# Second mixer: score groups issued between the two halves of a state drive, on other rows of the array

## Chip, core and metric

One core of a Trainium2 chip runs the whole program. The metric is the device time of one execution in microseconds, lower is better. TensorE (PE) does the matrix products, VectorE (DVE), ScalarE (ACT) and GpSimd (POOL) the element work, and SyncE (SP) issues the loads of the weights.

## What is computed

Two transformer layers with 256 tokens and width 1024 (`first_block`), then a third layer (`second_block`), all in float32. The change is in the mixer of the third layer, which has three branches over one input `h`:

```python
qa, ka, va, u, qm, km, vm, gates = split_in(h @ w_in[l])
oa = swa_attention(qa, ka, va, sinks[l], slopes_swa)       # 8 heads of 64, 2 key heads
ys = s5_ssm(u, ...)                                        # 32 groups x 64 complex states
om = moba_attention(qm, km, vm, slopes_moba)               # 8 heads of 64, 2 key heads
mixed = g[0] * (oa @ w_o_swa) + g[1] * (glu(gelu(ys)) @ w_o_ssm) + g[2] * (om @ w_o_moba)
```

In the state branch each group drives 64 complex states from 16 inputs. Two groups fill 128 partitions of states, so the 32 groups make 16 blocks. A block's drive is a product over 32 rows (two groups of 16 inputs), once for the real and once for the imaginary part. A scan over the 256 tokens follows, and a product over 128 rows that projects the states back.

## The kernel before

**Weights.** Every weight is loaded as `raw`, rounded by ACT to `whi` (L1029), and the rest is formed by DVE as `wlo` (L1563). PE then runs three products for each (L432, L433, L434). A piece is 1024 columns of one weight; DVE and ACT prepare a piece two ahead of PE (`AHEAD`), in three buffers.

**The strips of the second mixer.** `MIXED` lists 40 pieces, s = 0 to 39: the keys, the queries, six gate matrices of four pieces each (`gate2` is s = 28 to 31, `gate3` s = 32 to 35) and the first output projection. Tables say at which s something else is done beside the piece, and PE, ACT, DVE and POOL each walk through s in order:

- `SCORED_AT`: an attention item, that is 4 heads of 128 x 128 scores or 2 heads of 128 x 256, in one PSUM bank (`score`, L553). Items 0 to 5 are of `sA`, 6 to 11 of `mA`. The heads of an item are all even or all odd, so that its products all read rows 0 to 63, or all rows 64 to 127. DVE adds the bias and takes the maximum (L1731 on), ACT takes exponentials (L1109), PE transposes them one strip later (`prob_turn`, L538), ACT copies them (L1122), and PE multiplies by the values three strips after the scores (`weigh`, L566).
- `DRIVEN_AT`: a block of the state (`drive`, L939), two products of 32 rows x 256 columns in one bank. Block jj of four reads rows 32 jj to 32 jj + 31. DVE multiplies by phases (`turn_back`, L2356 and L2357), POOL adds (L2576 and L2577), DVE scans and multiplies at the next strip (`turn_forth`), POOL adds again, and PE projects four strips after the drive (`project`, L951).
- `ZIN_AT`: at s = 30 ACT takes the gelu of the first three quarters of the state branch's output (L1476, L1479).

Scores stand at odd s (7 to 29) and drives at even s (2 to 32). A turning bank of three (b3 to b5) takes scores, drives and transposes in turn; the strips use b0 to b2, two at a time, so that the second bank of a new strip group is the first bank of the one before: ACT must have emptied it (L1440 for a gate) before PE's fourth product of the new group.

The phases are built once, early in the program, by POOL (`phase_table`, L2509 and on): four blocks at a time, in DRAM until they are needed.

A float32 product like L553 or L939 is two instructions on PE in the trace (one for each half of the numbers), and the trace names the shape of the array that it uses: `64*128` is 64 rows by 128 columns.

The first mixer has a place where 64-row products on the two halves of the array follow each other: its differential scores (`diff_score`, L724), first the two or four products on rows 0 to 63, then those on rows 64 to 127. After the first of these groups comes a transpose of an 8-row tile on rows 0 to 7 (L749), array shape 32 x 128.

Of the kernel before, what the change touches and what calls it, by code (L numbers as in the profile page):

```python
# [13 lines left out]
P = 128  # L14
# [301 lines left out]

STRIP_END = {name: s + 1 for s, (name, n) in enumerate(MIXED)}

SCORED_AT = {7 + 2 * i: i for i in range(12)}
DRIVEN_AT = {2 + 2 * k: k for k in range(16)}  # L320
SWA_OUT, MOBA_OUT = 22, 34

ZIN_AT = {30: (0, 1, 2), 37: (3,)}
LAM_INIT = 0.8 - 0.6 * math.exp(-0.3 * 0)
# [75 lines left out]
def pe_program(K, G, A):  # L400

    S, T = K.S, K.nc.tensor
    pe = Engine(T)
    ident, banks = K.ident, K.banks
    free = [()] * 8
# [136 lines left out]
    def probs_ready(name, i):  # L542
        pe.wait_ge(*S.copied_a.at(("p", name, i)))

    def score(a, i, ready):
        t, heads = ITEMS[i]
        nk = P * (t + 1)
        b = turn_bank()
        K.place["s", a.name, i] = b
        for event in ready:  # L550
            pe.wait_ge(*event)
        for k, h in enumerate(heads):
            ins = T.matmul(banks[b][:, k * nk:(k + 1) * nk], a.queries(h, t), a.keys(h, nk), start=True, stop=True)  # L553
        ins.then_inc(*S.scored.done((a.name, i)))
        free[b] = (S.biased.at((a.name, i)),)
# [317 lines left out]
    def second():  # L873
        pairs[0], pair_n[0] = ((1, 2), (0, 1), (2, 0)), 1
        gemm("su", S.copied_d.at(("su", 0)), S.copied_d.at(("su", 1)), None, {0: lambda: norm_turns("s", "f3", True, (2, 3))})
        b = turn_bank()
        K.place["spread"] = b
        for t in range(2):
            pe.wait_ge(*S.rstd.at(("s", t)))
            ins = T.matmul(banks[b][:, P * t:P * t + P], K.stat(("y", "s"), 2)[:, t:t + 1].to_broadcast([P, P]), ident,  # L880
                           start=True, stop=True)
        ins.then_inc(*S.turned.done("spread"))
        free[b] = (S.copied_a.at("spread"),)

        def keys_piece(name, n):

            if n == 0:
                K.place[name] = next_pair()
            pair = K.place[name]
            hi, lo, j = piece("w_in_2", 0, 4 * n, 4, [({"ka": 512, "km": 1792}[name], 256)])  # L890
            K.at[name, n] = j
            for kk in range(4):
                kt = 4 * n + kk
                open_bank(pair[0])
                ins = products(banks[pair[0]][:, 0:256], (hi[:, kk, 0:P], lo[:, kk, 0:P]), wide(K.hT)(kt), kt == 0, kt == 7)
                if kt == 7:
                    ins.then_inc(*S.dense.done((name, 0)))
            for kk in range(4):
                kt = 4 * n + kk
                open_bank(pair[1])  # L900
                for t in range(2):
                    ins = products(banks[pair[1]][:, P * t:P * t + P], both(K.hT)(kt, t), (hi[:, kk, P:256], lo[:, kk, P:256]),
                                   kt == 0 and t == 0, kt == 7, True)
            ins.then_inc(*S.dense.done(("w", j), *([(name, 1)] if n else [])))
            if n:
                free[pair[0]], free[pair[1]] = (S.copied_d.at((name, 0)),), (S.copied_a.at((name, 1)),)

        def mixed_piece(name, n):
            if name in ("ka", "km"):
                keys_piece(name, n)  # L910
                return
            gemm_piece(G[name], n)
            if n == G[name].n - 1:
                for t in range(2):
                    free[K.place[name][t]] = ((S.gate.at((int(name[4]), t)) if name[:4] == "gate" else
                                               S.gated.at((0, int(name[3]), t)) if name[:3] == "swa" else S.copied_a.at((name, t))),)

        def ready(i):
            q, k = ("sqm", "km") if i >= 6 else ("sqa", "ka")
            return list(copied(q)) + [S.copied_d.at((k, 0)), S.keys[k].at(0)], [S.copied_a.at((k, 1))]  # L920

        def outputs_turn(J):
            b = turn_bank()
            K.place["out", J] = b
            pe.wait_ge(*S.cl.at(0))
            for ri in range(2):
                ins = T.transpose(banks[b][:, P * ri:P * ri + P], K.CL[ri][:, J, :], ident)
            ins.then_inc(*S.turned.done(("out", J)))
            free[b] = (S.proj.at(J),)

        def drive(k):
            J, jj = divmod(k, 4)
            b = turn_bank()
            K.place["drive", k] = b
            for t in range(2):
                pe.wait_ge(*S.copied_d.at(("su", t)))
            pe.wait_ge(*S.bt.at(1))
            for ri in range(2):
                ins = T.matmul(banks[b][:, 256 * ri:256 * ri + 256], K.BT[32 * jj:32 * jj + 32, ri, J, :],  # L939
                               K.uT[32 * jj:32 * jj + 32, J, :], start=True, stop=True)  # L940
            ins.then_inc(*S.driven.done(k))
            free[b] = (S.back.at(k),)

        def project(k):
            J, jj = divmod(k, 4)
            if jj == 0:
                open_bank(6)
            pe.wait_ge(*S.proj.at(J))
            pe.wait_ge(*S.turned_forth.at(k))
            for ri in range(2):  # L950
                ins = T.matmul(banks[6][:, 0:256], K.CR[:, J % 2, ri, P * jj:P * jj + P], K.state[k % 3][:, ri, :],  # L951
                               start=(jj == 0 and ri == 0), stop=(jj == 3 and ri == 1))
            ins.then_inc(*S.projected.done(k))
            if jj == 3:
                free[6] = (S.scan.at(("z", J)),)
                if J + 2 < 4:
                    outputs_turn(J + 2)
        for s, (name, n) in enumerate(MIXED):
            if s in SCORED_AT:
                i = SCORED_AT[s]  # L960
                score(A["mA" if i >= 6 else "sA"], i % 6, ready(i)[0])
            if s in DRIVEN_AT:
                drive(DRIVEN_AT[s])
            mixed_piece(name, n)
            if s == 1:
                outputs_turn(0)
                outputs_turn(1)
            if s - 4 in DRIVEN_AT:
                project(DRIVEN_AT[s - 4])
            if s - 3 in SCORED_AT:  # L970
                i = SCORED_AT[s - 3]
                weigh(A["mA" if i >= 6 else "sA"], i % 6, ready(i)[1])
            if s - 1 in SCORED_AT:
                i = SCORED_AT[s - 1]
                prob_turn("mA" if i >= 6 else "sA", i % 6, 4)
            if s in (SWA_OUT, SWA_OUT + 1):
                out_turn("sA", 0, K.O, lambda t, g: S.weighed.at(("sA", t)), (s - SWA_OUT,))
            if s in (MOBA_OUT, MOBA_OUT + 1):
                out_turn("mA", 0, K.O, lambda t, g: S.weighed.at(("mA", t)), (s - MOBA_OUT,))

        def gated(branch):
            return [[S.gated.at((branch, c, t)) for t in range(2)] for c in range(2)]
        pairs[0] = ((2, 0), (1, 3))
        gemm("glu1", S.silu.at(("glu", 0)), S.silu.at(("glu", 1)))
        gemm("glu0", S.product.at(("glu", 0)), S.product.at(("glu", 1)))
        gemm("moba0", *gated(2)[0])
        gemm("ssm0", *gated(1)[0])

        def out_of(c, g):
            out_turn(f"s{c}", 512 * c, K.M, lambda t, g: S.gated.at((1, c, t, g)), (g,))  # L990
        gemm("moba1", *gated(2)[1], None, {1: lambda: out_of(0, 0)})
        gemm("ssm1", *gated(1)[1], None, {0: lambda: out_of(0, 1)})
        project_x("s", "so", "f4", (0, 1, 2, 3), {1: lambda: out_of(1, 0), 2: lambda: out_of(1, 1)})
# [555 lines left out]
def dve_program(K, G, A):  # L1549
# [298 lines left out]
    SM = K.SM  # L1848
# [441 lines left out]
    def second():  # L2290
# [67 lines left out]

        def turn_forth(k):
            X, T = K.state[k % 3], K.spin[k % 2]  # L2360
            mg = SM[:, 1, k:k + 1].to_broadcast([P, 256])
            dve.wait_ge(*S.turned_back.at(k))
            if k:
                dve.wait_ge(*S.forth.at(k - 1))
            for a in range(2):
                V.tensor_tensor_scan(K.G[:, a, :], mg, X[:, a, :], 0.0, ALU.mult, ALU.add).then_inc(*S.dve_own.done())
            before()
            c, s = phases(k)
            V.tensor_tensor(T[:, 0], K.G, c, ALU.mult).then_inc(*S.dve_own.done())
            V.tensor_tensor(T[:, 1], K.G, s, ALU.mult).then_inc(*S.forth.done(k))  # L2370
# [102 lines left out]
def pool_program(K, G, A):  # L2473
# [28 lines left out]
    def phase_table(J):  # L2502
# [3 lines left out]
        if J >= 2:  # L2506
            pool.wait_ge(*S.spilled[J - 2].at(0))
        for ri in range(2):
            E.tensor_copy(tab[:, ri, :, 0:1], K.SM[:, 2 + ri, 4 * J:4 * J + 4].unsqueeze(2)).then_inc(*S.pool_own.done())  # L2509
        n = 1  # L2510
        while n < 256:
            c, s = tab[:, 0, :, 0:n], tab[:, 1, :, 0:n]
# [196 lines left out]
```

## Time and profile before

| | |
|---|---|
| median of 3 runs | 1677.44 us (1676.97 to 1677.71) |
| the profiled execution, its own time | 1676.27 us |
| its span in the trace | 1674.8 us |
| PE busy, share of the span | 99% |
| DVE, ACT, POOL | 66%, 52%, 14% |
| granted TensorE clock | 0.997 |
| second mixer in the trace | about 1250 to 1440 us |

A busy PE here means that some product was in the pipeline. Products overlap in the trace, since each stays in the pipeline after the next has begun; so the cost of one is read from the distance between the starts of two, not from its length.

### The profile page before, as it was taken

To read this page: it belongs to the slowest core of one execution; us is meant where nothing else is said; L and a number is where in the kernel's file an instruction comes from. 1 tells how busy PE (TensorE), PEld (TensorE's weight loads), DVE (VectorE), ACT (ScalarE), POOL (GpSimd) and SP (SyncE) were. 2 spreads that over 40 slices of the span, in tenths; PEclk is the share of its full clock that TensorE was granted. 3 is DMA by queue.
4 is the path that set the end of the run, shared out by engine and by line. 5 is a ranking of instruction groups with operands and counts; after the bars stand their busy time and mean duration, and the time that the engine had idled before them with its cause. 6 is when DMAs were issued, how large, how long until landed. Compare 5 with 4: busy or idle time off the path is not lost.

```text
span 1674.8 us, 21348 instructions
## 1 busy us (share of the span) xinstructions
PE 1652.0 (99%) x8136; PEld 1376.2 (82%) x8136; DVE 1102.3 (66%) x1744; ACT 864.4 (52%) x1323; POOL 236.4 (14%) x343
## 2 busy tenths in 40 slices
PE   7999999999999999999999999999999999999997
PEld 6888887788888888888889888888898778888886
DVE  5766788767656556555776685655568887775555
ACT  5555457665555445444544555544444446454444
POOL 2499701000000000000000000000044343100000
PEclk9999999999999999999999999999999999999999
DMA  8666755444455565655654453555574434555552
GB/s 250 203 214 202 228 158 186 144 140 138 146 195 179 187 187 177 189 188 189 201 163 141 162 162 123 183 187 189 188 237 141 134 120 136 187 191 189 189 180 97
DMA packets 185248, 293.05 MB, mean 175 GB/s; under 512 B 13527, under 2 KB 106234, under 8 KB 184250
## 3 DMA queue, kind: packets, MB, share of 16 engines
q1 hardware_dynamic: 180288, 274.81, 51.2%
q0 software_dynamic: 4368, 16.29, 3.1%
q8 instruction: 64, 1.05, 0.2%
q10 hardware_dynamic: 490, 0.59, 0.1%
q14 instruction: 38, 0.31, 0.1%
HBM read 286.12 MB, written 5.25 MB: 174 GB/s over the span
## 4 chain that ended last, share of the span: by engine, by line
PE 93%; DVE 4%; ACT 2%; issue 1%; ACTq 0%; DVEq 0%
PE b L432 28%; PE b L434 27%; PE b L433 27%; PE b L590 2%; PE b L553 1%; DVE wlo L1563 1%; PE b L566 1%; PE b L496 1%; PE b L939 1%; PE b L800 1%; PE b L951 1%; PE b L816 1%; PE b L538 1%; PE b L512 1%; ACT whi L1029 1%
## 5 line engine op out<-in xcount | busy, mean ns | idle before, releaser
L1563 DVE TENSOR_TENSOR wlo<-raw,whi 128x1024 fp32r<-128x1024 f32 (+1 forms) x523 | 653.3, 1252 | 465.3 <-ACT whi L1029 464.6
L1029 ACT ACTIVATE whi<-raw 128x1024 fp32r<-128x1024 f32 (+1 forms) x523 | 550.1, 1053 | 578.8 <-PE b L434 576.2
L432 PE MATMUL b<-whi,hT 128*128 128x512 f32 (+1 forms) x1184 | 468.9, 396 | 1.9 <-DVE wlo L1563 1.9
L434 PE MATMUL b<-whi,hT 128*128 128x512 f32 (+1 forms) x1184 | 459.0, 388 | 0.0
L433 PE MATMUL b<-wlo,hT 128*128 128x512 f32 (+1 forms) x1184 | 458.1, 387 | 0.0
L432 PEld LDWEIGHTS b<-whi,hT 128*128 128x128 f32 x1184 | 222.8, 188 | 53.1 <-issue 7.1
L432 PE MATMUL b<-whi,oT 128*128 128x512 f32 x672 | 264.8, 394 | 0.0
L434 PE MATMUL b<-whi,oT 128*128 128x512 f32 x672 | 261.9, 390 | 0.0
L433 PE MATMUL b<-wlo,oT 128*128 128x512 f32 x672 | 261.5, 389 | 0.0
L434 PEld LDWEIGHTS b<-whi,hT 128*128 128x128 f32 x1184 | 222.7, 188 | 46.7
L433 PEld LDWEIGHTS b<-wlo,hT 128*128 128x128 f32 x1184 | 223.1, 188 | 42.2 <-issue 0.5
L434 PEld LDWEIGHTS b<-whi,oT 128*128 128x128 f32 x672 | 126.1, 188 | 26.6
L433 PEld LDWEIGHTS b<-wlo,oT 128*128 128x128 f32 x672 | 126.3, 188 | 25.5
L432 PEld LDWEIGHTS b<-whi,oT 128*128 128x128 f32 x672 | 126.2, 188 | 25.4
L1109 ACT ACTIVATE R<-R,st 128x256 f32<-128x256 f32 (+1 forms) x96 | 43.5, 455 | 69.7 <-DVE st L1736 30.4
L2601 POOL DMA_DIRECT2D biasB<-in_rel x1 | 0.9, 917 | 494.9 <-PE b L590 494.9
L1156 ACT ACTIVATE biasA<-b,st 128x256 f32<-128x256 f32 x88 | 41.1, 475 | 44.1 <-PE b L434 42.8
L432 PE MATMUL b<-hT,whi 128*128 128x256 f32 (+1 forms) x216 | 62.8, 291 | 0.0
L433 PE MATMUL b<-hT,whi 128*128 128x256 f32 (+1 forms) x216 | 61.0, 282 | 0.0
L434 PE MATMUL b<-hT,wlo 128*128 128x256 f32 (+1 forms) x216 | 61.0, 282 | 0.0
L1644 DVE TENSOR_TENSOR oT<-b,oT 128x512 fp32r<-128x512 f32 x80 | 53.5, 683 | 9.4 <-ACT oT L1131 5.0
L2553 POOL DMA_DIRECT2D biasA<-in_alibi x1 | 0.5, 540 | 407.2 <-DVE biasB L1811 407.2
(315 smaller groups left out, 1782.2 us busy)
## 6 DMA issues: line engine op xcount, KB each, us to landing
raw<-in_ffn_w_in SPq DMA_DIRECT2D x350, 256.0 KB, 3.0
raw<-in_ffn_w_out SPq DMA_DIRECT2D x88, 512.0 KB, 3.3
raw<-in_w_ff SPq DMA_DIRECT2D x64, 512.0 KB, 3.3
raw<-in_w_in SPq DMA_DIRECT2D x40, 512.0 KB, 3.6
raw<-in_x_w_kv SPq DMA_DIRECT2D x32, 512.0 KB, 3.5
raw<-in_even_w_in SPq DMA_DIRECT2D x24, 512.0 KB, 4.1
raw<-in_odd_w_in SPq DMA_DIRECT2D x24, 512.0 KB, 3.8
raw<-in_x_w_q SPq DMA_DIRECT2D x16, 512.0 KB, 3.9
```

Source lines behind the costliest of these rows:

```text
L432: T.matmul(out, ah, bh, start=start, stop=False, skip_group_check=skip)
L433: T.matmul(out, ah, bl, start=False, stop=False, skip_group_check=skip)
L434: return T.matmul(out, al, bh, start=False, stop=stop, skip_group_check=skip)
L496: ins = T.transpose(banks[b][:, (2 * i + t) * P:(2 * i + t + 1) * P], src[:, t, kt * P:(kt + 1) * P], ident)
L512: ins = T.transpose(banks[b][:, i * P:(i + 1) * P], K.sqj[t][:, i * P:(i + 1) * P], ident)
L538: ins = T.transpose(banks[b][:, k * P:(k + 1) * P], src[:, k * P:(k + 1) * P], ident)
L590: ins = T.transpose(banks[b][:, (2 * i + t) * P:(2 * i + t + 1) * P], K.fa[(2 * c + t) % 4][:, col:col + P], ident)
L1029: E.activation(K.whi[j % NSPLIT][:, 0:n], K.raw[j % NRAW][:, 0:n], ACT.Copy).then_inc(*S.whi.done(j))
L1109: ins = E.activation(s3[:, h, :], s3[:, h, :], ACT.Exp, bias=nm[:, h:h + 1], accum_out=sm[h])
L1156: ins = E.activation(s[:, 0:256], bank[:, 0:256], ACT.Silu, scale=rs)
L1563: V.tensor_tensor(K.wlo[j % NSPLIT][:, 0:n], K.raw[j % NRAW][:, 0:n], K.whi[j % NSPLIT][:, 0:n].bitcast(F32), ALU.subtract).then_inc(*S.wl ...
L1644: V.tensor_tensor(lo, src, hi.bitcast(F32), ALU.subtract).then_inc(*S.alo.done(key))
```

## The change

Scores move from odd strips to even ones (8 to 30), to the strips at which the drives stand. In a strip that has both, the drive's first product is issued ahead of the first head, and its second product ahead of the middle head. Blocks of the state are taken in the order 0, 2, 1, 3, in the drive, the projection, the decay and the phase table; with it every drive that is paired reads rows of the half of the array that its score item doesn't read.

```diff
-SCORED_AT = {7 + 2 * i: i for i in range(12)}
+SCORED_AT = {8 + 2 * i: i for i in range(12)}
 DRIVEN_AT = {2 + 2 * k: k for k in range(16)}
-SWA_OUT, MOBA_OUT = 22, 34
+SWA_OUT, MOBA_OUT = 23, 35
+
+BLOCKS = (0, 2, 1, 3)
...
         for k, h in enumerate(heads):
+            if k in beside:
+                beside[k]()
             ins = T.matmul(banks[b][:, k * nk:(k + 1) * nk], a.queries(h, t), a.keys(h, nk), start=True, stop=True)
...
-        def drive(k):
-            J, jj = divmod(k, 4)
-            b = turn_bank()
-            K.place["drive", k] = b
+        def drive_open(k):
+            K.place["drive", k] = turn_bank()
             for t in range(2):
                 pe.wait_ge(*S.copied_d.at(("su", t)))
             pe.wait_ge(*S.bt.at(1))
-            for ri in range(2):
-                ins = T.matmul(banks[b][:, 256 * ri:256 * ri + 256], K.BT[32 * jj:32 * jj + 32, ri, J, :],
-                               K.uT[32 * jj:32 * jj + 32, J, :], start=True, stop=True)
-            ins.then_inc(*S.driven.done(k))
-            free[b] = (S.back.at(k),)
+
+        def drive(k, ri):
+            J, jj = k // 4, BLOCKS[k % 4]
+            b = K.place["drive", k]
+            ins = T.matmul(banks[b][:, 256 * ri:256 * ri + 256], K.BT[32 * jj:32 * jj + 32, ri, J, :],
+                           K.uT[32 * jj:32 * jj + 32, J, :], start=True, stop=True)
+            if ri:
+                ins.then_inc(*S.driven.done(k))
+                free[b] = (S.back.at(k),)
...
         for s, (name, n) in enumerate(MIXED):
+            k = DRIVEN_AT.get(s)
+            if k is not None:
+                drive_open(k)
             if s in SCORED_AT:
-                i = SCORED_AT[s]
-                score(A["mA" if i >= 6 else "sA"], i % 6, ready(i)[0])
-            if s in DRIVEN_AT:
-                drive(DRIVEN_AT[s])
+                i, half = SCORED_AT[s], len(ITEMS[SCORED_AT[s] % 6][1]) // 2
+                score(A["mA" if i >= 6 else "sA"], i % 6, ready(i)[0],
+                      {} if k is None else {0: lambda: drive(k, 0), half: lambda: drive(k, 1)})
+            elif k is not None:
+                drive(k, 0)
+                drive(k, 1)
             mixed_piece(name, n)
...
         for ri in range(2):
-            E.tensor_copy(tab[:, ri, :, 0:1], K.SM[:, 2 + ri, 4 * J:4 * J + 4].unsqueeze(2)).then_inc(*S.pool_own.done())
+            for i, block in enumerate(BLOCKS):
+                E.tensor_copy(tab[:, ri, i, 0:1], K.SM[:, 2 + ri, 4 * J + block:4 * J + block + 1]).then_inc(*S.pool_own.done())
```

The order on PE, before, at strips 15 and 16 of the mixer, where a score of two heads stands ahead of one piece (b4 takes the scores):

```order
L566 MATMUL b7<-R1 128x64 x4
L538 MATMUL b3<-cst,R1 128x128 x4
L553 MATMUL b4<-R1 128x256 x2
L432 MATMUL b0<-whi0,hT0 128x512
L433 MATMUL b0<-wlo0,hT0 128x512
L434 MATMUL b0<-whi0,hT1 128x512
```

and the drive stands between two later pieces (b5 takes it):

```order
L434 MATMUL b1<-whi0,hT1 128x512
L939 MATMUL b5<-vsb,BT 128x256 x2
L432 MATMUL b2<-whi1,hT0 128x512
L433 MATMUL b2<-wlo1,hT0 128x512
L434 MATMUL b2<-whi1,hT1 128x512
```

After the change, PE's order in that part of the mixer, where `drive` is L945, `score` L558 and the three products are L434 to L436 (the new file's lines):

```order
L571 MATMUL b7<-R1 128x64 x4
L540 MATMUL b3<-cst,R1 128x128 x4
L945 MATMUL b4<-vsb,BT 128x256
L558 MATMUL b5<-R1 128x256
L945 MATMUL b4<-vsb,BT 128x256
L558 MATMUL b5<-R1 128x256
L434 MATMUL b2<-whi1,hT0 128x512
L435 MATMUL b2<-wlo1,hT0 128x512
L436 MATMUL b2<-whi1,hT1 128x512
```

A 64-row and a 32-row product now alternate, and the strip between two such groups has neither. The other place is ACT near strip 30, before the change: the exponentials of item 11 (L1109) come one weight ahead of the gelu (L1476), and the evacuation of `gate2` (L1440) after it.

```order
L1122 ACTIVATE R1<-b3 128x512
L1109 ACTIVATE R1,st<-R1,st 128x256 x2
L1029 ACTIVATE whi2<-raw1 128x1024
L1476 ACT_TABLE_LOAD
L1476 ACTIVATE vsb<-vsb 128x256 x3
L1479 ACTIVATE mT0<-vsb 128x256 x3
L1029 ACTIVATE whi0<-raw2 128x1024
L1122 ACTIVATE R1<-b3 128x512
L1440 ACT_TABLE_LOAD
L1440 ACTIVATE biasB<-b2,st 128x512
```

and after it, with the same work at L1134, L1121, L1041, L1488, L1491 and L1452:

```order
L1041 ACTIVATE whi2<-raw1 128x1024
L1134 ACTIVATE R1<-b3 128x512
L1121 ACTIVATE R1,st<-R1,st 128x256 x2
L1488 ACT_TABLE_LOAD
L1488 ACTIVATE vsb<-vsb 128x256 x3
L1491 ACTIVATE mT0<-vsb 128x256 x3
L1041 ACTIVATE whi0<-raw2 128x1024
L1452 ACT_TABLE_LOAD
L1452 ACTIVATE biasB<-b2,st 128x512
```

The exponentials belong to a score that PE issues one strip later than before, while the gelu, the weight behind it and the evacuation keep their strips.

## Rows read from the trace of the kernel before

**Rows 1.** The page: span, busy time of each engine
```profile
span 1674.8 us, 21348 instructions
PE 1652.0 (99%) x8136; PEld 1376.2 (82%) x8136; DVE 1102.3 (66%) x1744; ACT 864.4 (52%) x1323; POOL 236.4 (14%) x343
```
**Rows 2.** What weight loads of PE waited for, 1260 to 1420 us (total, times, longest)
```profile
PEld b L432 <- ACT R L1440: 0.4, 1, 0.4
```
**Rows 3.** Timeline of PE around a drive: start us, length us, instruction, count
```profile
1336.49 0.39 PE L433 MATMUL b<-wlo,hT 128*128 128x512 f32 x1
1336.71 0.39 PE L434 MATMUL b<-whi,hT 128*128 128x512 f32 x1
1337.03 1.12 PE L939 MATMUL b<-vsb,BT 32*128 32x256 f32 x4
1338.09 0.50 PE L432 MATMUL b<-whi,hT 128*128 128x512 f32 x1
1338.42 0.39 PE L433 MATMUL b<-wlo,hT 128*128 128x512 f32 x1
```
**Rows 4.** The chain: a projection, whose neighbours use the same array shape
```profile
1320.77 0.86 PE b L951 x4
```
**Rows 5.** Timeline of PE around a score item of two heads
```profile
1322.31 0.61 PE L538 MATMUL b<-cst,R 128*128 128x128 f32 x4
1322.85 1.13 PE L553 MATMUL b<-R 64*128 64x256 f32 x4
1323.90 0.50 PE L432 MATMUL b<-whi,hT 128*128 128x512 f32 x1
```
**Rows 6.** Timeline of PE at a differential score of the first mixer, both halves
```profile
277.10 1.14 PE L724 MATMUL b<-R 64*128 64x256 f32 x8
278.17 0.50 PE L432 MATMUL b<-whi,hT 128*128 128x512 f32 x1
```
**Rows 7.** Timeline of PE where rows 64 to 127 are followed by rows 0 to 7
```profile
267.39 0.27 PE L724 MATMUL b<-R 64*128 64x128 f32 x1
267.59 0.28 PE L749 MATMUL b<-cst,M 8*128 8x8 f32 x2
267.81 0.50 PE L432 MATMUL b<-whi,hT 128*128 128x512 f32 x1
```
**Rows 8.** Timeline of POOL: the issue that waited for the data that L749 turns
```profile
263.73 0.53 POOL L2535 DMA_DIRECT2D cum<-M  x1 [60.70 <-DVE M L2017]
```
**Rows 9.** POOL's copies in the phase table: min, median, max ns, first and last start
```profile
L2509 POOL COPY R<-SM x8: 186/211/277, 65.9 to 169.6; 128x4 f32<-128x4 f32 x8
```
**Rows 10.** Timeline of DVE: the low halves prepared after the score of rows 5
```profile
1327.40 1.22 DVE L1563 TENSOR_TENSOR wlo<-raw,whi 128x1024 fp32r<-128x1024 f32 x1
```
**Rows 11.** Timeline of PE: the piece that uses them
```profile
1334.08 0.50 PE L432 MATMUL b<-whi,hT 128*128 128x512 f32 x1
```
**Rows 12.** Timeline of PE: item 11, drive 14, fourth product of strip 32
```profile
1384.97 1.13 PE L553 MATMUL b<-R 64*128 64x256 f32 x4
1388.97 1.12 PE L939 MATMUL b<-vsb,BT 32*128 32x256 f32 x4
1399.73 0.40 PE L432 MATMUL b<-whi,hT 128*128 128x512 f32 x1
```
**Rows 13.** Timeline of DVE: bias and maximum of item 11, the drive's first product
```profile
1386.71 0.74 DVE L1731 SCALAR_TENSOR_TENSOR R<-b,st,biasB 128x512 f32<-128x512 f32 x1
1390.19 0.69 DVE L2356 TENSOR_TENSOR R<-b,M 128x512 f32<-128x512 f32 x1 [0.88 <-issue]
```
**Rows 14.** Timeline of ACT: exponentials, gelu, next weight, evacuation of gate2
```profile
1388.21 0.51 ACT L1109 ACTIVATE R<-R,st 128x256 f32<-128x256 f32 x1 [2.54 <-DVE st L1736]
1390.27 1.28 ACT L1476 ACT_TABLE_LOAD   x1
1393.43 1.04 ACT L1029 ACTIVATE whi<-raw 128x1024 fp32r<-128x1024 f32 x1
1397.31 1.37 ACT L1440 ACTIVATE biasB<-b,st 128x512 f32<-128x512 f32 x2 [0.18 <-PE b L434]
```

More of the change, by code:

```diff
@@ L543, in probs_ready, with score @@
         pe.wait_ge(*S.copied_a.at(("p", name, i)))
-    def score(a, i, ready):
+    def score(a, i, ready, beside={}):
         t, heads = ITEMS[i]
@@ L937, in drive @@
             pe.wait_ge(*S.bt.at(1))
-            for ri in range(2):
-                ins = T.matmul(banks[b][:, 256 * ri:256 * ri + 256], K.BT[32 * jj:32 * jj + 32, ri, J, :],
-                               K.uT[32 * jj:32 * jj + 32, J, :], start=True, stop=True)
-            ins.then_inc(*S.driven.done(k))
-            free[b] = (S.back.at(k),)
+        def drive(k, ri):
[6 more added lines that the diff above has]
+                free[b] = (S.back.at(k),)
         def project(k):
-            J, jj = divmod(k, 4)
-            if jj == 0:
+            J, jj = k // 4, BLOCKS[k % 4]
+            if k % 4 == 0:
                 open_bank(6)
@@ L951, in project @@
                 ins = T.matmul(banks[6][:, 0:256], K.CR[:, J % 2, ri, P * jj:P * jj + P], K.state[k % 3][:, ri, :],
-                               start=(jj == 0 and ri == 0), stop=(jj == 3 and ri == 1))
+                               start=(k % 4 == 0 and ri == 0), stop=(k % 4 == 3 and ri == 1))
             ins.then_inc(*S.projected.done(k))
-            if jj == 3:
+            if k % 4 == 3:
                 free[6] = (S.scan.at(("z", J)),)
@@ L2360, in turn_forth @@
             X, T = K.state[k % 3], K.spin[k % 2]
-            mg = SM[:, 1, k:k + 1].to_broadcast([P, 256])
+            block = 4 * (k // 4) + BLOCKS[k % 4]
+            mg = SM[:, 1, block:block + 1].to_broadcast([P, 256])
             dve.wait_ge(*S.turned_back.at(k))
```

## The prediction

> **What bounds the kernel now.** I read the page first: PE is busy 1652.0 of 1674.8 us, the others at most 66% [rows 1]. Then the waits of PE in the second mixer, where all of the change on PE lies. Weight loads there wait for other engines once for 0.4 us [rows 2], and hardly at all besides. So the mixer takes what PE's own instructions take, and the change is worth what it does to the distances between the starts of PE's products. For that I read PE's timeline around a drive and around a score item.
>
> **What a block of small products costs now.** Ordinary products start 0.22 to 0.23 us apart (1336.49, 1336.71). From the last of them to the first drive product it is 0.32 us, the four drive instructions take 1.06 us until the next ordinary product starts, and this one's follower starts 0.33 us later instead of 0.23 [rows 3]. Four instructions of the same 256 columns without a change of array shape take 0.86 us [rows 4]. So a drive costs 0.09 + 1.06 + 0.10 = 1.25 us, of which 0.86 is streaming, and 0.39, about 0.20 for each of its two changes of shape (128 rows to 32, and back). The 0.20 has two parts: some 0.09 in which nothing starts, and 0.10 for weights that were not loaded ahead.
>
> A score item costs the same. Its four instructions take 1.05 us to the next ordinary product [rows 5]; the four transposes before it start 0.54 us ahead, where 0.11 us each (half of the 0.215 of rows 4) would be 0.44. I use 1.25 us for it, again with two changes (128 to 64, and back).
>
> **What the change does on PE.** No product is added or removed. Of 16 drives, 12 (blocks 3 to 14) now share a strip with a score item, in the order drive, score, drive, score. What this costs hangs on one thing: whether a product of 32 rows and one of 64 rows, on different rows of the array, run at once, or whether going from one to the other is a change of shape like those above.
>
> The trace has a case for each part of it. Two 64-row groups on different halves do run at once: eight instructions of 256 columns take 1.07 us [rows 6], as long as four take elsewhere. So float32 products can overlap by rows. But the shape there is the same on both sides. Where the shape differs, there is one place: the last 64-row product on rows 64 to 127 starts at 267.39, and the first 32-row one, on rows 0 to 7, at 267.59 [rows 7]. An instruction of 128 columns streams for 0.11 us, so 0.09 us passed with nothing starting: the same pause as at 128 to 32. Its data can't be what it waited for: they were there at 263.73 at the latest, when POOL, which waits for the same data, went on [rows 8]. So rows that don't overlap did not save the pause when the shape changed.
>
> I take this as the rule. A pair then has five changes of shape (128, 32, 64, 32, 64, 128) where the two blocks apart had four. One more change for each of 12 pairs is 12 x 0.20 = +2.4 us, and nothing overlaps. The bound above: if 32 and 64 rows do overlap, a pair costs what the block of rows 6 does, 1.07 + 0.19 = 1.26 us, in place of 1.25 + 1.25, so 12 x 1.24 = 14.9 us less. A bound below for one change: a pause alone, without the weight load, is 0.09, so +1.1 us.
>
> The Trainium skill speaks against the change too: its page "TensorEngine Tiling (Array Packing)", section "Key Properties", says that changing the tiling mode, and not only the tile, drains TensorE. By that rule alone the gain of 14.9 us would be none and the loss of the size that I give; the trace agrees at the one place of rows 7, in one direction.
>
> **What it does elsewhere, costed at nothing.**
> - POOL's phase tables: eight one-column copies in place of two, for four tables: 24 more at about 0.21 us [rows 9] and no wait for anything, 5 us. POOL waits 60.7 us after the tables [rows 8], which covers it twelve times.
> - DVE has the same work in another order: bias and maximum now follow `turn_back` at even strips, not `turn_forth` at odd ones. The low halves of a piece are ready at 1328.6 and used at 1334.08 [rows 10, 11], 5.5 us early, more than the 3 us by which anything moves. POOL's additions between the two turns now lie beside the bias, and DVE, which is no bound, waits less.
> - The time from scores to their transposes gets shorter by about one drive, 1.2 us, and the bias starts earlier behind two products than behind `turn_forth`. In item 11 the exponentials start 3.2 us after the scores and take 1.0 [rows 12, 14], while two pieces of 12 products of 0.23 us, 5.5 us, and the weighing lie ahead of the transposes.
> - The strips' gate banks are emptied by ACT beside exponentials that now start later in the same strip, behind the evacuation; there the wait of rows 2 may go, 0.4 us at most.
>
> One place is tight. At strip 30 the exponentials of item 11 stand ahead of the gelu, the next weight and the evacuation of `gate2` on ACT. Now they start at 1388.21 and take 1.0 (two of 0.51), the gelu starts at 1390.27 behind another weight, the weight 1393.43, the evacuation 1397.31, and its first half (0.69 of the 1.37) ends at 1398.0 [rows 14]; PE's fourth product at strip 32, which opens that bank, starts at 1399.73 [rows 12], 1.7 us later. After the change: drive 14 would start at 1388.97, plus 11 x 0.20 for the pairs before it, minus 1.25 for item 11, which is no longer ahead: 1389.9. DVE's first product begins 1.22 after the drive's start today [rows 12, 13], 2.05 after it in a pair, 1391.95. Its two products take 1.3, bias and maximum 1.5 (1386.71 to 1388.21, rows 13 and 14), so the exponentials start at 1394.7 and end at 1395.7. Gelu with table load 3.2, weight 1.0, table load of the evacuation 1.5 and its first half 0.7 give 1402.1. PE asks for it at 1399.73 + 2.4 = 1402.1. So there is nothing left of the 1.7 us, and no wait to speak of either, within about 1 us.
>
> **The sum.** +2.4 us. On the profiled execution's own 1676.27 us (span 1674.8) that is 1678.7 and a span of 1677.2; on the median, 1677.44, which stands 1.2 us above the profiled one, 1679.8 us, +0.14%. What a measurement of this kernel can tell from no change is about 0.2%, 3.4 us. I forecast a loss that is smaller than that.
>
> **The rivals.**
> 1. Full overlap. A 32-row drive and a 64-row score on the other half run together as in rows 6. For it: overlap of rows exists on this chip, in float32, and rows 7 is a single place, 64 to 32. Against it: that place. Time 1677.4 - 14.9 = 1662.5. In the profile a pair would take 1.1 us. The skill's page "TensorE: Matmul & The Clock Gate", part 3, "Packing small matmuls", would give this: it lets products on different row groups overlap and says nothing of their sizes.
> 2. Overlap from 32 to 64, a pause from 64 to 32. The trace has no place that goes from 32 to 64. Each pair then has two overlapped couples and three changes: 2 x 0.86 - 0.86 = 0.86 and one change, 0.20, less, 1.06 x 12 = 12.7 us; 1664.7.
> 3. Slower beyond what is told apart. The chain on ACT at strip 32 comes late: each us by which the exponentials of item 11 are later than I worked out is a us of PE's wait. It takes 1 us, that is exponentials starting after 1395.7, to bring the loss to 3.4 us and over the bound. For it: there is no slack left by my sum, and DVE may not be free when the drive lands. Against it: nothing in the sum is rounded down, and one wait of 0.4 us may go. Time 1681 to 1682.5.
> 4. The pairs cost nothing: if the pause hides the weight load, +1.1 us, 1678.5; within the forecast's own range.
>
> **Chances.** The forecast, with 4, 0.68 (1678 to 1681); rival 1 0.13; rival 2 0.06; rival 3 0.13. Below 1674.1 (faster by 0.2%) lie rivals 1 and 2: 0.19. Above 1680.8 lie rival 3 and the upper edge of the forecast, 0.07: together 0.20. Same: 0.61. The range leaves out rivals 1 and 2, 0.19, and takes in the bound of one change below and a wait of 3 us at strip 32 above: 1677.3 to 1683.
>
> **What would show it.** In a pair of the changed kernel I look for five distances of 0.30 to 0.32 us, one at each change of shape, and eight instructions in 2.5 us until the next ordinary product (8 x 0.215 + 5 x 0.20, less the 0.19 that lie outside). If the first score instruction starts 0.01 us behind the first drive instruction, rival 1 or 2 is right. The waits of weight loads at 1402 show rival 3. A span under 1670 us would make the prediction wrong in its main step.

## The result and the profile after

| | before | changed |
|---|---|---|
| median of 4 runs | 1677.38 us (1676.97 to 1677.71) | 1686.33 us (1684.67 to 1687.88) |
| ratio | | 1.0055 (1.0043 to 1.0068) |
| the profiled execution, its own time | 1676.27 us | 1687.88 us |

The change costs 9 us in the median, and 11.6 us in the profiled execution. The forecast was +2.4 us. The page of the changed kernel, to be read beside [rows 1]:

```profile
span 1686.4 us, 21383 instructions
PE 1660.0 (98%) x8136; PEld 1379.4 (82%) x8136; DVE 1093.5 (65%) x1744; ACT 864.2 (51%) x1323; POOL 238.9 (14%) x367
```

PE has the same 8136 instructions and is busy 8.0 us longer, and there are another 3.6 us in which it is not. Where in the program do they arise? I take one stretch, from the mixer's first projection to the first product that reads `mT`, in the output projection behind the mixer. Timeline of PE before, its two ends:

```profile
1269.50 1.08 PE L951 MATMUL b<-O,R 128*128 128x256 f32 x4
1425.39 0.28 PE L432 MATMUL b<-mT,whi 128*128 128x256 f32 x1
```

and after, the same two:

```profile
1270.16 1.08 PE L958 MATMUL b<-O,R 128*128 128x256 f32 x4
1436.98 0.28 PE L434 MATMUL b<-mT,whi 128*128 128x256 f32 x1
```

The stretch was 155.89 us and is 166.82, so 10.93 of the 11.6 us arise in the mixer. This difference, called **the stretch** below, is the measure of every experiment too, because the rest of the program varies by about as much as a small effect (runs of the kernel before went from 1674.8 to 1680.6 us on the chips used here). It is always taken against the 155.89 us of this one profile of the kernel before; run 6 below, whose stretch should not differ from it, comes within 0.01 us.

**A pair.** Timeline of PE at one pair of drive and score:

```profile
1319.04 0.61 PE L540 MATMUL b<-cst,R 128*128 128x128 f32 x4
1319.57 0.69 PE L945 MATMUL b<-vsb,BT 32*128 32x256 f32 x2
1320.20 0.70 PE L558 MATMUL b<-R 64*128 64x256 f32 x2
1320.82 0.69 PE L945 MATMUL b<-vsb,BT 32*128 32x256 f32 x2
1321.45 0.70 PE L558 MATMUL b<-R 64*128 64x256 f32 x2
1322.07 0.50 PE L434 MATMUL b<-whi,hT 128*128 128x512 f32 x1
1322.41 0.39 PE L435 MATMUL b<-wlo,hT 128*128 128x512 f32 x1
```

This is what the forecast said. Eight instructions take 2.50 us (1319.57 to 1322.07). Two of them take 0.63, where two without a change of shape take 0.43 (half of [rows 4]): 0.20 at each change, from 32 to 64 rows and from 64 to 32 alike. No drive product runs beside a score product.

**Strip 24.** The chain of work that ended last, start, length and what it was:

```profile
1361.44 0.45 PE b L526 x4
1361.89 0.02 issue
1361.92 0.60 ACT oT L1080
1362.51 0.94 ACT whi L1041
1363.46 0.50 ACT R L1134
1363.95 0.14 issue
1364.09 0.67 PE b L945 x2
1364.75 0.63 PE b L558 x2
1365.38 0.88 PE b L945 x2
1366.26 1.15 PE b L558 x2
1367.40 0.72 PE b L434
1368.13 0.43 PE b L435
```

Here the chain leaves PE for three pieces of ACT. PE's output transposes (L526) are done at 1361.89, and the drive starts at 1364.09. The list of PE's waits (total, times, longest) has the same 2.2 us:

```profile
PE b L945 <- ACT R L1134: 2.2, 1, 2.2
```

From 1365.38 on everything on PE takes longer: two score instructions 1.15 in place of 0.63, an ordinary product 0.43 in place of 0.23. The windows say why. Columns: stretch, its length, busy time of PE, of its weight loads, of DVE, ACT and POOL (with instructions begun), granted clock (PEclk), DMA share, GB/s.

```profile
1276.00:1283.00 7.00, 7.00 (x31) 6.14 (x32) 5.45 (x10) 3.94 (x11) 2.70 (x5) 0.56 0.34 97
1358.00:1365.00 7.00, 4.79 (x29) 3.84 (x28) 4.90 (x7) 5.27 (x12) 2.33 (x2) 1.00 0.49 135
1365.00:1372.00 7.00, 7.00 (x17) 4.49 (x16) 5.64 (x9) 1.09 (x4) 1.42 (x2) 0.54 0.16 30
1372.00:1379.00 7.00, 7.00 (x38) 5.60 (x37) 2.58 (x4) 3.20 (x4) 2.54 (x4) 0.97 0.55 167
```

The clock was granted at its lower level, 1.2 of 2.4 GHz, for 6.8 us from about 1365.6 on, 1.5 us behind the end of the wait, and for another 6.8 us from about 1276.9 on, at the first pair (strip 8), where PE waited for nothing. I call this a fall of the clock. The kernel before has 1.00 in the same windows:

```profile
1276.00:1283.00 7.00, 7.00 (x49) 6.16 (x50) 5.30 (x9) 3.89 (x10) 3.44 (x4) 1.00 0.56 171
1365.00:1372.00 7.00, 7.00 (x30) 5.08 (x29) 6.90 (x11) 2.40 (x6) 2.50 (x4) 1.00 0.41 137
```

What does a fall cost? I compare the same part of the program with and without one. From the first projection to that of strip 8 the changed kernel takes 13.56 us here and 10.58 in run 1 below, which has no fall there: 2.98 us. From the projection of strip 20 to that of strip 26 it takes 37.62 us, and 32.23 in run 2 below, which has neither wait nor fall in these strips: 5.39 us, of which the wait is 2.2 and the clock 3.2. That leaves 10.93 - 2.98 - 5.39 = 2.56 us for the new order of the products, near the forecast's 2.4. The other 8.4 us stand in no term of it.

**Where the wait comes from.** PE's order at strip 24, with bank numbers:

```
L571 MATMUL b7<-R1 128x64 x4
L540 MATMUL b4<-cst,R1 128x128 x4
L526 MATMUL b5<-cst,O 128x128 x4
L945 MATMUL b3<-vsb,BT 128x256
L558 MATMUL b4<-R1 128x256
L945 MATMUL b3<-vsb,BT 128x256
L558 MATMUL b4<-R1 128x256
```

There are three turning banks, and four tenants (users of a bank) follow in a row: transposed probabilities (b4), output transposes (b5), drive (b3), and the score, which is back at b4. Both banks of a pair are opened ahead of the first drive product, so the drive waits until ACT has copied the probabilities out of b4. On ACT that copy (L1134) stands behind a half of the outputs (L1080) and a weight (L1041). At all other pairs no output transposes come between, and the score gets a bank whose former tenant lies at least a piece back. In the kernel before, the next tenant of the probabilities' bank was another output transpose, one whole piece of products later.

### The profile page after: what moved, and what is told of

Same layout as the page of the kernel before. It is cut to its first block, busy times and chain, and to the rows that moved or that the text cites. A ratio compares the mean times of both kernels' runs of the same rounds, so it can differ in the third digit from the quotient of the medians.

```text
span 1686.4 us, 21383 instructions
## 1 busy us (share of the span) xinstructions
PE 1660.0 (98%) x8136; PEld 1379.4 (82%) x8136; DVE 1093.5 (65%) x1744; ACT 864.2 (51%) x1323; POOL 238.9 (14%) x367
## 4 chain that ended last, share of the span: by engine, by line
PE 92%; DVE 4%; ACT 2%; issue 1%; ACTq 0%; DVEq 0%
PE b L434 27%; PE b L436 27%; PE b L435 27%; PE b L595 2%; PE b L558 1%; DVE wlo L1575 1%; PE b L945 1%; PE b L571 1%; PE b L498 1%; ACT whi L1041 1%; PE b L805 1%; PE b L958 1%; PE b L821 1%; PE b L540 1%; PE b L514 1%
## 5 line engine op out<-in xcount | busy, mean ns | idle before, releaser
L1041 ACT ACTIVATE whi<-raw 128x1024 fp32r<-128x1024 f32 (+1 forms) x523 | 550.1, 1054 | 580.9 <-PE b L436 578.4
L434 PE MATMUL b<-whi,hT 128*128 128x512 f32 (+1 forms) x1184 | 470.9, 398 | 2.5 <-DVE wlo L1575 2.5
L436 PE MATMUL b<-whi,hT 128*128 128x512 f32 (+1 forms) x1184 | 459.9, 388 | 0.0
L434 PEld LDWEIGHTS b<-whi,hT 128*128 128x128 f32 x1184 | 223.4, 189 | 50.8 <-issue 4.1
L434 PE MATMUL b<-whi,oT 128*128 128x512 f32 x672 | 264.9, 394 | 0.0
L436 PE MATMUL b<-whi,oT 128*128 128x512 f32 x672 | 261.9, 390 | 0.0
L436 PEld LDWEIGHTS b<-whi,hT 128*128 128x128 f32 x1184 | 223.2, 189 | 47.1
L436 PEld LDWEIGHTS b<-whi,oT 128*128 128x128 f32 x672 | 126.1, 188 | 26.7
L434 PEld LDWEIGHTS b<-whi,oT 128*128 128x128 f32 x672 | 126.2, 188 | 25.7 <-DVE R L2330 0.5
L1121 ACT ACTIVATE R<-R,st 128x256 f32<-128x256 f32 (+1 forms) x96 | 43.6, 456 | 81.8 <-DVE st L1748 40.0
L434 PE MATMUL b<-hT,whi 128*128 128x256 f32 (+1 forms) x216 | 64.2, 297 | 0.0
L436 PE MATMUL b<-hT,wlo 128*128 128x256 f32 (+1 forms) x216 | 62.0, 287 | 0.0
```

What stands on the lines that cost most here:

```text
L434: T.matmul(out, ah, bh, start=start, stop=False, skip_group_check=skip)
L436: return T.matmul(out, al, bh, start=False, stop=stop, skip_group_check=skip)
L1041: E.activation(K.whi[j % NSPLIT][:, 0:n], K.raw[j % NRAW][:, 0:n], ACT.Copy).then_inc(*S.whi.done(j))
L1121: ins = E.activation(s3[:, h, :], s3[:, h, :], ACT.Exp, bias=nm[:, h:h + 1], accum_out=sm[h])
```

## Experiments

My theory: the rule of the forecast holds (0.20 us for each change of shape, no overlap of 32 with 64 rows), and the loss beyond it is the wait of strip 24 and the clock behind it, plus a fall of the clock at a pair. "Before" in a result is the median of the kernel before on the same chip, and the ratio is to it. Rivals: the wait is the fall's consequence or an accident of one execution; the falls come from the alternation itself; 32 and 64 rows can't overlap because of their place, and not their size.

### 1. The changed kernel again

No edit.

> The changed kernel once more, for a second profile. The one profile of it shows, beside the alternation of array shapes, a wait of 2.3 us ahead of drive 11 at strip 24, a granted clock of 0.5 for 6.8 us right after it, and the same at 1276.6 us, behind the first pair, where nothing waited. Theory A (the loss beyond the alternation comes from the wait at strip 24 and from clock drops, of which some come and go between executions): the wait is there again, 2.3 us, and so is the alternation; the number of drops may differ; the median is 1684 to 1688. Theory B (the alternation itself costs more than 0.2 us a pair, everywhere): the distance between the two kernels grows evenly over the 12 pairs.

Measured: 1684.52 us (1684.35 to 1685.01), before 1676.94; ratio 1.0044 (1.0031 to 1.0058). The chain shows the same three pieces of ACT from 1358.69 to 1360.73 ahead of the drive. Windows:

```profile
1276.00:1283.00 7.00, 7.00 (x52) 6.32 (x51) 5.83 (x11) 4.67 (x12) 2.50 (x5) 1.00 0.34 100
1361.00:1368.00 7.00, 7.00 (x16) 4.07 (x17) 4.33 (x6) 1.09 (x4) 1.42 (x2) 0.55 0.15 55
```

The wait and the clock behind it are there again, the fall at strip 8 is not. The projection of strip 8, in the first profile and in this one, 13.56 and 10.58 us behind the first projection (1270.16 and 1269.93):

```profile
1283.72 1.03 PE L958 MATMUL b<-O,R 128*128 128x256 f32 x4
1280.51 1.03 PE L958 MATMUL b<-O,R 128*128 128x256 f32 x4
```

The stretch is +7.95 us. Strips 22 to 26 hold 5.36 of it (by comparison with run 2), which leaves 2.6. Theory B, even growth over the pairs, is wrong: up to the projection of strip 20, with seven of the twelve pairs, the growth is 1.13 us. The two groups of the first four executions fit this: 1684.67 and 1684.98 at a mean clock of 0.997, 1687.67 and 1687.88 at 0.995 and 0.994, 3.0 us apart, the price of one fall.

### 2. Both output transposes at strip 24, behind the pair

```diff
-SWA_OUT, MOBA_OUT = 23, 35
+SWA_OUT, MOBA_OUT = 24, 35
...
-            if s in (SWA_OUT, SWA_OUT + 1):
-                out_turn("sA", 0, K.O, lambda t, g: S.weighed.at(("sA", t)), (s - SWA_OUT,))
+            if s == SWA_OUT:
+                out_turn("sA", 0, K.O, lambda t, g: S.weighed.at(("sA", t)))
```

> The changed kernel, but both transposes of the sliding-window branch's output are issued at strip 24 (with their copies at strip 25), so that no drive opens a bank whose transposes were issued just before it. Theory A: no wait at strip 24 and no clock drop after it: 2.3 + 3.4 us less than the profile of the changed kernel where it had both; the median comes to before plus the alternation, 1679 to 1681.5. Theory B: the kernel stays at 1684 or more.

Measured: 1682.89 us (1682.25 to 1683.79); 1.0034 (1.0022 to 1.0047). The chain at strip 24 stays on PE:

```profile
1361.79 0.62 PE b L945 x2
1362.41 0.63 PE b L558 x2
```

So the order of the banks made the wait, and without the wait no fall stands there. But this execution has the fall at strip 8 (granted clock 0.58 over 1276 to 1283), and its way from the first projection to that of strip 8 is 3.00 us longer than in run 1. The stretch is +5.58, which leaves 2.6.

### 3. As 2, with the drive whole ahead of the score

```diff
-                      {} if k is None else {0: lambda: drive(k, 0), half: lambda: drive(k, 1)})
+                      {} if k is None else {0: lambda: (drive(k, 0), drive(k, 1))})
```

> As the run with both transposes at strip 24, but both products of the drive are issued before the first head, so that a pair has three changes of array shape (128 to 32, 32 to 64, 64 to 128) and not five. My price of 0.20 us for a change: 12 x 2 x 0.20 = 4.8 us under the run with transposes at strip 24, and 2.4 us under before, 1675. The rival, that 32-row and 64-row products overlap partly when they alternate, would make this one slower than that run. A third possibility, that pauses cost nothing, would leave it equal.

Measured: 1677.11 us (1674.12 to 1679.44, 11 runs); 0.9999 (0.999 to 1.0008). Timeline of a pair, now with three changes of shape:

```profile
1326.32 1.12 PE L945 MATMUL b<-vsb,BT 32*128 32x256 f32 x4
1327.37 1.13 PE L558 MATMUL b<-R 64*128 64x256 f32 x4
1328.43 0.50 PE L434 MATMUL b<-whi,hT 128*128 128x512 f32 x1
```

2.11 us in place of 2.50: two changes fewer, 0.20 each. The stretch is -2.17 us, where one change fewer than before for each of 12 pairs is -2.4. The price per change holds for fewer changes as for more. The median doesn't show the 2.2 us; the interval reaches from -1.7 to +1.3 us, and run 9 below shows that such pairs can meet a fall of the clock as well.

### 4. The drive on 64 rows, so that both shapes are alike

The drive reads its own 32 rows and the other 32 of the same half, whose weights belong to another block. Its result is therefore that of two blocks added up: this kernel computes another state.

```diff
+            rows = slice(64 * (jj // 2), 64 * (jj // 2) + 64)
-            ins = T.matmul(banks[b][:, 256 * ri:256 * ri + 256], K.BT[32 * jj:32 * jj + 32, ri, J, :],
-                           K.uT[32 * jj:32 * jj + 32, J, :], start=True, stop=True)
+            ins = T.matmul(banks[b][:, 256 * ri:256 * ri + 256], K.BT[rows, ri, J, :],
+                           K.uT[rows, J, :], start=True, stop=True)
```

> As the run with both transposes at strip 24, but each drive's product reads the 64 rows of its half of the array, not its 32, so that drive and score have one array shape and lie on different halves. It leaves out that the other block's 32 rows would need zero weights: the states get the other block's inputs added, and the output is not the reference's; the instructions are those that a right version would have. Theory A with the rule of shapes: the two overlap as the differential scores do; a pair takes 1.07 us until the next ordinary product in place of 2.5, 12 x 1.43 = 17 us under the run with transposes at strip 24: 1662 to 1665. Rival: the score's products don't start beside the drive's in this order (another bank, another stationary operand each time): 1675, as with three changes less.

Measured: 1662.57 us (1661.85 to 1666.55); 0.992 (0.9907 to 0.9932). Timeline of a pair:

```profile
1332.27 0.48 PE L946 MATMUL b<-vsb,BT 64*128 64x256 f32 x1
1332.28 0.48 PE L558 MATMUL b<-R 64*128 64x128 f32 x2
...
1333.36 0.50 PE L434 MATMUL b<-whi,hT 128*128 128x512 f32 x1
```

A drive and a score product start 0.01 us apart, and the whole pair takes 1.09 us until the next ordinary product. The stretch is -13.96. It is the shape, 32 against 64 rows, and not the place or the order that kept them apart.

### 5. The drive on 64 rows, with padded weights

Here the state is that of the reference again. Each block's weights are padded with zeros to the 64 rows of its half. GpSimd writes the padded weights to DRAM early in the program and loads them back for four blocks at a time, in two buffers. The core of it:

```diff
-            pe.wait_ge(*S.bt.at(1))
+            pe.wait_ge(*S.btl[k // 4 % 2].at(k // 4))
...
+            rows = slice(64 * (jj // 2), 64 * (jj // 2) + 64)
-            ins = T.matmul(banks[b][:, 256 * ri:256 * ri + 256], K.BT[32 * jj:32 * jj + 32, ri, J, :],
-                           K.uT[32 * jj:32 * jj + 32, J, :], start=True, stop=True)
+            ins = T.matmul(banks[b][:, 256 * ri:256 * ri + 256], K.BTz[rows, J % 2, ri, jj % 2, :],
+                           K.uT[rows, J, :], start=True, stop=True)
```

> The run with the drive on 64 rows, now whole: each block's weights lie in SBUF with zeros in the other block's 32 rows, in two buffers of four blocks each; GpSimd brings them from DRAM, where they are put with their zeros at about 310 us, when it is idle. PE's instructions are those of the run with the drive on 64 rows. If nothing of the loads is late: its time, 1661.9 to 1666.5, at any rate more than 10 us under before. Rival: GpSimd's issues at strips 8 and 16 (0.55 us each) delay its additions, so that scans and projections come late: one more wait of up to 1 us at two places.

Measured: 1663.71 us (1662.86 to 1664.63), before 1676.83 on that chip; 0.992 (0.9906 to 0.9933). Timeline of a pair:

```profile
1319.59 0.48 PE L951 MATMUL b<-vsb,BT 64*128 64x256 f32 x1
1319.60 0.48 PE L563 MATMUL b<-R 64*128 64x256 f32 x1
```

The stretch is -13.94, as in 4, so the loads cost nothing there. This version is 13 us faster than the kernel before.

### 6. The kernel before, with drives of 64 rows, apart from the scores

The edit of 4 in the kernel before (again a state of two blocks added up).

> The kernel before with one change: each drive's product reads the 64 rows of its half, not 32 (the partner block's weights are not zeroed, so the states get its inputs added). Drives and scores stand apart as before. Overlap theory: the gain of the run with the drive on 64 rows comes from the two running together, so this one is equal to before, 1677 within 0.2%. Rival: a 64-row product is itself cheaper than a 32-row one, or its change of shape is: then this gains too, 16 drives x up to 0.4 us = 6 us.

Measured: 1677.37 us (11 runs), before 1676.83; 1.0004 (0.9996 to 1.0013). The stretch is +0.01 us. A wider drive alone neither costs nor gains; all of the gain of 4 and 5 is the overlap.

### 7. The changed kernel, with the copy of the probabilities first at strip 24

```diff
+            if s - 2 in SCORED_AT and s == SWA_OUT + 1:
+                i = SCORED_AT[s - 2]
+                probs("mA" if i >= 6 else "sA", i % 6)
...
-            if s - 2 in SCORED_AT:
+            if s - 2 in SCORED_AT and s != SWA_OUT + 1:
```

> The changed kernel, but at strip 24 ScalarE copies the transposed probabilities ahead of the output's half and the next weight, not behind them. If the wait ahead of drive 11 is for the bank of these transposes, it falls from 2.3 us to about 0.6; if the clock drop behind it comes of PE's standing still, it goes too: 1684.5 - 1.7 - 3.4 = 1679.4. If the drop has another cause: 1682.8. If the wait is for something else: 1684.5.

Measured: 1683.2 us (1680.28 to 1686.95, 4 runs); 1.0043 (1.0028 to 1.0059). Chain, PE's waits and windows of the profiled execution, the fastest of the four:

```profile
1358.83 0.61 ACT R L1134
1359.44 0.14 issue
1359.57 0.67 PE b L945 x2
```

```profile
PE b L945 <- ACT R L1134: 0.3, 1, 0.3
```

```profile
1349.00:1353.00 4.00, 4.00 (x13) 3.12 (x13) 3.90 (x10) 0.00 (x0) 1.42 (x2) 0.63 0.24 92
1357.00:1361.00 4.00, 3.66 (x24) 2.71 (x23) 1.72 (x2) 3.27 (x5) 2.30 (x2) 1.00 0.55 167
```

The chain has one copy in place of three pieces. It starts when the probabilities are transposed, and PE transposes outputs (L526) beside it for most of its time, so that PE waits 0.3 us, and no fall follows. A fall stands at strip 22 instead, where nothing waited. The stretch is +4.50. From the projection of strip 20 to that of strip 26 it is 1.95 us longer than in run 2: 0.3 for the wait and some 1.6 for the shorter fall, 3.4 us at the lower level. The median does not show that the wait went: the four executions differ by 6.7 us, and 1683.2 is nearer to the 1682.8 expected for a fall with another cause than to 1679.4. What shows it is the trace of strip 24.

### 8. As 2, with the drive whole at the first pair alone

Only the pair at strip 8 has three changes of shape; the others alternate. A test of whether the alternation there brings the fall.

> The run with both transposes at strip 24, but in the first pair (strip 8) the drive is issued whole ahead of the score, so that this pair has three changes of shape and not five; the other 11 alternate. That run's profile has a clock drop of 6.8 us from 1276.9, in its first pair, with nothing waited for, and its mixer takes 5.6 us more than before's, of which my alternation explains 2.4. If the pauses of the first pair bring on the drop: no drop, and 1682.9 - 0.4 - 3 = 1679.5. If the drop comes at that place for another reason, or from chance: 1682.5.

Measured: 1681.93 us (1680.37 to 1685.34, 8 runs); 1.003 (1.002 to 1.004). The clock fell at strip 8 all the same:

```profile
1275.00:1279.00 4.00, 4.00 (x27) 3.41 (x27) 2.96 (x5) 2.75 (x4) 3.52 (x5) 0.93 0.54 163
1279.00:1283.00 4.00, 4.00 (x24) 3.97 (x24) 3.83 (x9) 1.86 (x11) 1.07 (x2) 0.64 0.18 40
```

It lasts 3.4 us here, and the way to the projection of strip 8 is 1.50 us longer than in run 3, which has the same pair there. The stretch of +3.65 leaves 2.15, and 11 changes more and one fewer are +2.0.

### 9. Drive whole ahead of the score, and the wait kept

The edit of 3 in the changed kernel, whose output transposes stay at strips 23 and 24.

> The changed kernel with both products of the drive ahead of the first head (three changes of shape in a pair), but with the output transposes left at strips 23 and 24. Theory: the wait at strip 24 comes from the rotation of the banks alone and the granted clock falls behind it whatever the pairs look like; so the chain shows some 2.3 us ahead of the drive of strip 24, the clock stands at 0.5 for some microseconds behind it, and the time is that of the run with whole drives and transposes at 24 (1677.1) plus 2.3 for the wait and 2 to 3.5 for the clock: 1681.5 to 1683. Rival: the clock falls because the pairs alternate, the wait only hastened it; then only the wait is added, 1679.4 us, and the clock stays at 1.

Measured: 1681.97 us (1679.54 to 1683.71, 9 runs), before 1677.41; 1.0027 (1.0017 to 1.0036). PE's waits, and two windows:

```profile
PE b L945 <- ACT R L1134: 2.2, 1, 2.2
```

```profile
1277.00:1281.00 4.00, 4.00 (x22) 3.77 (x22) 3.82 (x8) 2.56 (x7) 2.13 (x4) 0.57 0.43 150
1359.00:1366.00 7.00, 6.15 (x13) 4.11 (x14) 3.33 (x5) 1.27 (x5) 1.42 (x2) 0.53 0.18 65
```

The wait and the fall at it are there with pairs that don't alternate. Here the clock fell at about 1359.4, 1.8 us into the wait (1357.6 to 1359.9) and not behind its end. The stretch is +4.62, 6.8 us over that of run 3. Compared part by part with run 3, strips 22 to 26 hold 5.27 of it, that is 2.2 for the wait and 3.1 for the clock, and strip 8 holds 1.5. So the rival, that it takes the alternation to lower the clock, is refuted twice, at strip 24 and at strip 8. Whether the alternation makes a fall more frequent is not shown.

### 10. Run 2 once more

> The kernel with the output transposes at strip 24 once more, for a second profile of pairs that alternate and have no wait. Theory: pairs with five changes of shape lower the clock now and then where nothing waits; in this profile the clock falls to 0.5 at least once between 1250 and 1440 us, not always at the same strip, and the time is 1682 to 1684. Rival: the fall at strip 8 in the first profile was an accident; here the mixer has none, its own growth is some 2.3 us, and the profiled execution takes about 1679.5.

Measured: 1682.21 us (1678.28 to 1686.91, 10 runs); 1.0027 (1.0017 to 1.0037). Strip 8 is undisturbed this time, and strip 22 is not:

```profile
1276.00:1283.00 7.00, 7.00 (x49) 5.94 (x48) 4.99 (x10) 4.01 (x10) 4.23 (x6) 1.00 0.32 95
1352.00:1356.00 4.00, 4.00 (x12) 3.21 (x12) 3.90 (x11) 0.00 (x1) 1.42 (x2) 0.60 0.20 75
```

The fall costs 1.6 us here (strips 22 to 26 against run 2), the stretch is +4.13, and 2.6 is left. Three of the ten executions took 1678.3 to 1679.6 us, about what the forecast gives for the new order alone; they have no profile.

## Why the prediction was wrong

- **The price of a block and of a change of shape** was right. After the falls and the wait are taken out, the stretch grows by 2.6 us in four profiles (the changed kernel twice, runs 2 and 10) against the forecast's +2.4; with one change fewer it shrinks by 2.2 (run 3) against -2.4. Some 0.4 us of both comes behind the last pair, where the output transposes of the other attention branch moved too. The pairs themselves grow by 2.15 us, 0.18 each, and shrink by 2.58 in run 3, 0.21 each: the 0.20 holds, and that the sum of the stretch is so near has a little luck in it.
- **No overlap of 32 with 64 rows** was right, in both directions. The forecast had taken it from one place whose second shape the trace writes as `8*128` [rows 7], not `32*128`; the pairs show it for 32 rows. Rival 1 and rival 2 were wrong for this change, and right about the chip where both sides have 64 rows: runs 4 and 5 gain 13.1 to 14.4 us in the median and 13.9 in the stretch, where rival 1 said 14.9. The Trainium skill's "TensorEngine Tiling (Array Packing)", "Key Properties", says that a change of tiling mode drains TensorE; the traces agree, with 0.20 us a change.
- **The step that failed** is the part "What it does elsewhere, costed at nothing". It followed the data (what is ready when) and the strips' banks, but not the turning banks. `SWA_OUT` moved by one strip and the scores moved by one strip, and together they put four tenants in a row into three banks at strip 24. Rival 3 named a wait of this kind, at strip 32 and with ACT's evacuation as its cause. No wait came there: in the changed kernel nothing on PE waits between 1380 and 1440 us. So the direction of rival 3 was right, but its place and its mechanism were not. That the wait of strip 24, 2.2 us, comes from the banks and from ACT's order is shown by runs 2 and 7, which take it away and cut it to 0.3 in two ways.
- **The sum lacked a term for the clock.** The wait brought a fall with it that costs more than itself: 3.2 us in the first profile and in run 1, 3.1 in run 9, and none at strip 24 where the wait was gone (runs 2, 3, 8 and 10) or cut to 0.3 us (run 7). For this kernel the wait's true price is 5.4 us. How long a wait it takes for that is not shown.
- **The falls at pairs where nothing waits** (strip 8 in the changed kernel and in runs 2, 8 and 9, strip 22 in runs 7 and 10) cost 1.5 to 3.0 us in the executions that have them. They are the likely reason why run 2 and run 10 stay at +5 to +6 us in the median and not at +2.4; only one execution of each has a profile. What brings them on stays open. That it takes the alternation is ruled out by run 8 and run 9. In no profile of the kernel before or of runs 3 to 6 did one stand in the mixer, but run 3 has the same kind of pair as run 9, so their absence from one profile proves little; pairs that share a strip in a 32-row and a 64-row shape, 3 to 5 changes close together, are what all executions with such a fall have in common. That is an observation, and no experiment isolates it.

So the median's +9.0 us is, to within what the measurement can tell, 2.6 for the new order, most of it the changes of shape, 2.2 for the wait, 3.2 for the clock behind it, and about 1.5 for the fall at strip 8: the profiled execution has it, at 3.0 us, and by its time one more of the four does. That makes 9.5. The forecast's direction was right by its one term; the larger part of the loss, 6.9 of the 9.5 us, comes from what it had at nothing.

## What to carry to other kernels

In these runs products on different rows of the array ran at once only where their shapes were alike. So pad the smaller one (13 us here, for a few loads) and don't alternate two sizes, which cost a change of shape each time. When work moves between steps of a program, write down the tenants of each rotating bank in the new order, and not only the time at which data are ready; where a bank comes back after fewer steps than before, find its emptier in the other engine's queue and add up what stands ahead of it. And on an engine that is never idle otherwise, price a wait of some 2 us with the clock that may fall behind it.

## What the runs showed of the hardware

- A wait of PE of 2.2 us came, three times out of three, with 6.8 us at the lower clock, which cost some 3 us more. The fall began 1.5 and 0.9 us behind the wait's end in two profiles and 1.8 us into the wait in the third (run 9). A wait of 0.3 us at the same place had none (run 7).
- The granted clock also fell with PE busy throughout, at a pair of small products, for 3.4 or 6.8 us, in some executions of a kernel and not in others. The shorter cost 1.5 to 1.6 us, the longer 3.0.
- Float32 products of 64 rows on the two halves of the array start 0.01 us apart, also when they belong to different work (a drive and a score). Between 32 and 64 rows each change cost 0.18 to 0.21 us, on different rows too and in either direction.
- A drive of 64 rows took as long as one of 32 (run 6: +0.01 us over the 13 drives of the stretch).
